# Residual stream in DRAM and a ring of five tiles in the norm stages, in place of a resident tensor

## The chip, the cores and the metric

One core of one Trainium2 chip runs one program. The metric is the device time of one execution in microseconds (us). A core has a matrix engine (TensorE, PE in the profile, with its weight loads as PEld), VectorE (DVE), ScalarE (ACT), GpSimd (POOL) and SyncE (SP), which here only issues DMAs. DMAs that SP issues are in queue q1 of the profile, the indirect gathers that GpSimd issues in queue q0, and both run on the same 16 DMA engines.

## The reference

Two layers of a diffusion backbone over 1024 latent and 256 context tokens of width 1024, all in float32. Cut to what matters here:

```python
for i in range(2):
    hl = modulate(rms_norm(xl, norm_mix[i]), mod_l[0], mod_l[1])   # hc from xc likewise
    yl, yc = neighbourhood_attention(hl, hc, ...) if i == 0 else diff_attention(hl, hc, ...)
    xl = xl + mod_l[2] * yl
    hl = modulate(rms_norm(xl, norm_ffn[i]), mod_l[3], mod_l[4])
    y = grouped_moe(hl, ...)                # layer 0: latent and context tokens, layer 1: latent only
    xl = xl + mod_l[5] * y
return rms_norm(xl, final_norm)
```

`xl` and `xc` together are the residual stream. It is touched in five places only: before each attention, after each attention (the branch is added, then the second norm), and after each mixture of experts, where the addition belongs to the next norm.

## The kernel before, in words

The tokens stand in tiles of 128 partitions by 1024 floats, 512 KB each: ten tiles in all, of which eight are latent. The residual stream `x_res` holds all ten tiles on chip from its allocation in `build` (L1599) to the end, 40 KB of every partition.

One function, `normed`, is called five times, each time as a block of its own with a barrier at its end:

- **Stage 1** (layer 0, mode mix, source None, ten tiles): loads the input into `x_res` and normalises it.
- **Stage 2** (layer 0, mode ffn, source project, ten tiles): projects the attention output, adds it to the stream, normalises, routes.
- **Stage 3** (layer 1, mode mix, source combine, ten tiles): gathers each token's two expert results, adds them, normalises.
- **Stage 4** (layer 1, mode ffn, source project, eight tiles): as stage 2.
- **Stage 5** (mode final, source combine, eight tiles): as stage 3, and the normalised rows are the output.

Between them stand attention, routing and the experts, which do not touch the stream.

Inside a stage every engine has its own written-out program over steps u. In step u, tile u gets its addition, tile u-1 its sum of squares and its 1/rms, tile u-2 its scaling and shift, and tile u-3 its transposes, tile u-4 its routing. The order on each engine:

- **SyncE** issues, in a combine stage, the gate rows (L346; two DMAs of 512 KB in stage 3, one in stage 5), then the norm rows (L360, four DMAs in stages 2 and 3, two in stage 4; L356, one, in stage 5). In an ffn stage `router_w` follows (L377, 64 KB in small pieces). In stage 3, once two tiles are squared, it issues three weight loads of the next attention (L299). In ffn and final stages it then stores each tile's normalised rows as they become ready (L382), and waits for these stores (L384).
- **TensorE**, in an ffn stage, waits for `router_w` and the output weights before its first instruction; then per step 16 matmul calls (L400, 32 in the profile's counts), the transposes (L412) and the router (L420). In stages 1 and 3 it runs four pieces of the next attention's projection between the transposes (L292).
- **VectorE**, in a combine stage, waits for the gate rows before anything. Per tile it combines the two expert rows (L476), multiplies by the gate (L478), adds the result to x (L480), and scales tile u-2 (L501). In an ffn stage it multiplies the projection by its gate (L488).
- **ScalarE** scales the first gathered row (L445), squares (L456) and evicts half of the transposes (L463).
- **GpSimd** issues two indirect gathers of 512 KB for each tile in a combine stage (L523), two tiles ahead, into three buffers; tile t's gather waits until tile t-3 is added. In an ffn stage it adds the two halves to x (L537). It computes 1/rms (L542, L544) and adds the shift (L551).

VectorE's program holds, in a combine stage:

```python
dve.wait_ge(s_gr, 16 * streams)                       # gate rows, before step 0
...
nc.vector.tensor_tensor(x[:, u, :], x[:, u, :], y0, ALU.add).then_inc(s_x, 1)
```

Of the kernel before, what the change touches and what calls it, by code (L numbers as in the profile page):

```python
# [116 lines left out]
def build(nc, a):  # L117
# [4 lines left out]
    h_dram = dram("h_rows", [NTOK, D])  # L122
    idx_dram = [dram(f"slot_token{l}", [SLOTS[l], 16], I32) for l in range(2)]
# [11 lines left out]
    def sb(c, name, shape, dt=F32):  # L135
        return c.enter_context(nc.sbuf_tensor(unique(name), shape, dt))
# [11 lines left out]
    with top:  # L148
# [152 lines left out]
        def normed(l, mode, T, source, hT=None, rw=None, attn=None, wq=None, w_in=None):  # L301
# [3 lines left out]
            with ExitStack() as c:  # L305
                junk = sb(c, "junk", [P, D])
                hr = sb(c, "hr", [P, 3, D])
                if mode == "ffn":
                    hT = sb(c, "h_tile_T", [P, KD, 2 * P])
# [4 lines left out]
                if source is None:  # L314
                    loads = ((0, 2), (2, 5), (5, LT), (LT, NT))
                    s_xin = [sem(c, f"x_in{n}") for n in range(len(loads))]
                    s_toep = sem(c, "toep_out")
                if mode != "final":
                    s_tr, s_eva, s_evd, s_rt, s_rw = (sem(c, n) for n in (
                        "h_transposed", "hT_low", "hT_high", "routed", "router_in"))  # L320
# [20 lines left out]

                @block.sync
                def _(sp):
                    if source == "combine":
                        for v in range(streams):
                            sp.dma_start(gate[:, v, :], mods[prev, v, 5 * D:6 * D].partition_broadcast(P)).then_inc(s_gr, 16)  # L346
# [31 lines left out]
                    if mode != "mix":  # L378
                        for t in range(T):
                            sp.wait_ge(s_h, t + 1)  # L380
                            dst = out[0, t * P:(t + 1) * P, :] if mode == "final" else h_dram[t * P:(t + 1) * P, :]
                            sp.dma_start(dst, hr[:, t % 3, :]).then_inc(s_st[t % 3], 16)  # L382
                        for n in range(3):
                            sp.wait_ge(s_st[n], 16 * len(range(n, T, 3)))  # L384
# [56 lines left out]
                def _(act):  # L441
                    for u in step_range:
# [3 lines left out]
                        if at(u, L_SQ):  # L446
                            t = u - L_SQ
                            if t:
                                act.wait_ge(s_ss, t)
                            if source is None:  # L450
                                for n, (t0, t1) in enumerate(loads):
                                    if t == t0:
                                        act.wait_ge(s_xin[n], 16)
                            else:
                                act.wait_ge(s_x, adds * (t + 1))
                            nc.scalar.activation(junk[:, :], x[:, t, :], ACT.Square, accum_out=ss[:, t:t + 1]).then_inc(s_ss, 1)  # L456
# [10 lines left out]
                def _(dve):  # L467
# [4 lines left out]
                    for u in step_range:  # L472
                        if source == "combine" and at(u, 0):
# [6 lines left out]
                            nc.vector.tensor_tensor(x[:, u, :], x[:, u, :], y0, ALU.add).then_inc(s_x, 1)  # L480
# [9 lines left out]
                        if at(u, L_SC):  # L490
# [10 lines left out]
                            nc.vector.scalar_tensor_tensor(out=hr[:, t % 3, :], in0=x[:, t, :], scalar=rstd[:, t:t + 1],  # L501
# [15 lines left out]
                def _(pool):  # L517
# [11 lines left out]
                    for u in step_range:  # L529
                        if source == "combine" and u + 2 < T:  # L530
                            gather(u + 2)
                        if source == "project" and at(u, 0):
                            for h in range(2):
                                n = 2 * u + h
                                pool.wait_ge(s_g, n + 1)
                                xs = x[:, u, h * HALF:(h + 1) * HALF]
                                nc.gpsimd.tensor_tensor(xs, xs, tmp[:, n % 4, :], ALU.add).then_inc(s_x, 1)  # L537
# [1061 lines left out]
        x = sb(top, "x_res", [P, NT, D])  # L1599
# [50 lines left out]
```

## Time and profile before

| | |
|---|---|
| median of 3 runs | 4670.02 us (4668.69 to 4672.05) |
| the profiled execution: its own time, its span | 4662.88 us, 4661.0 us |
| TensorE busy, mean granted clock | 4244.4 us (91%), 0.956 of full speed |
| VectorE, ScalarE, GpSimd busy | 1412.5, 979.4, 516.2 us |
| DMA | 628.09 MB, mean 135 GB/s over the span |
| stage 1 | 182 to 251 us |
| stage 2 | 1166 to about 1350 us |
| stage 3 | 2427.5 to 2534 us |
| stage 4 | 3481 to 3633 us |
| stage 5 | 4604.8 to 4661 us |

Times inside the span are counted from its first instruction. A row of the timeline gives the start and the length of an instruction or of several merged ones, the engine (SPq is SyncE's queue of DMA issues), the line, what it writes and reads, and in brackets how long the engine had been idle and what ended that. The granted clock is a share of 2.4 GHz: 0.50 is the lower of the two levels.

### The profile page before, as it was taken

The numbers are of one execution on the slowest core, as the hardware profiler recorded it, in microseconds if no ns is written. First come the engines' busy times: TensorE is split into PE (matmuls) and PEld (weight loads), VectorE is DVE, ScalarE is ACT, GpSimd is POOL, SyncE is SP. The second block draws the span as 40 slices with busy tenths as digits, with TensorE's granted clock in tenths as the row PEclk, the third lists the DMA queues.
The fourth block names the chain that finished last, engine by engine and source line by source line (L and its number), as shares of the span: only waits on it lengthen the run. The fifth ranks groups of instructions, "written<-read, shape, count | busy, mean of one in ns | idle before, by whom it ended". The sixth has DMA issues, their size and how long they took to land. (4 is left out here: it accounts for less than half of the span.)

```text
span 4661.0 us, 61468 instructions
## 1 busy us (share of the span) xinstructions
PE 4244.4 (91%) x25164; PEld 3369.6 (72%) x25164; DVE 1412.5 (30%) x2522; ACT 979.4 (21%) x2014; POOL 516.2 (11%) x492
## 2 busy tenths in 40 slices
PE   7799999999967999999975999999989499999994
PEld 2377777777446789999973666666664489999994
DVE  6643333334131101111116444444441311111113
ACT  4433333333000000000112333333331000000102
POOL 0220000000231000000005000000003200000002
PEclk9899999999978999999997999999999699999997
DMA  8770000001135345778852000000010555579894
GB/s 312 247 291 22 22 21 21 21 21 46 37 137 161 128 145 183 240 262 272 294 199 87 14 14 13 13 13 13 13 51 23 186 173 192 196 244 299 296 300 167
DMA packets 468239, 628.09 MB, mean 135 GB/s; under 512 B 30432, under 2 KB 343280, under 8 KB 467928
## 3 DMA queue, kind: packets, MB, share of 16 engines
q1 hardware_dynamic: 439512, 529.33, 34.9%
q0 software_dynamic: 22240, 73.58, 4.4%
q10 hardware_dynamic: 6312, 22.55, 1.2%
q8 instruction: 146, 2.39, 0.2%
q14 instruction: 29, 0.24, 0.0%
HBM read 558.39 MB, written 70.95 MB: 135 GB/s over the span
## 5 line engine op out<-in xcount | busy, mean ns | idle before, releaser
L1507 PE MATMUL ps<-item_xT,expert_ring 128*128 128x128 f32 (+9 forms) x8192 | 1169.6, 306 | 1.1 <-DVE item_xT L1573 1.1
L1507 PEld LDWEIGHTS ps<-item_xT,expert_ring 128*128 128x128 f32 x8192 | 1114.4, 192 | 51.8 <-DVE item_xT L1573 1.4
L1529 PE MATMUL ps<-item_aT,expert_ring 128*128 128x128 f32 (+9 forms) x4096 | 620.2, 307 | 0.0
L1529 PEld LDWEIGHTS ps<-item_aT,expert_ring 128*128 128x128 f32 x4096 | 567.2, 192 | 25.1 <-issue 1.8
L292 PE MATMUL ps<-hT,w_group 128*128 128x512 f32 (+1 forms) x1408 | 532.0, 537 | 6.0 <-ACT df_probs L1092 3.9
L292 PEld LDWEIGHTS ps<-hT,w_group 128*128 128x128 f32 x1408 | 265.7, 191 | 255.1 <-issue 242.7
L1580 DVE TENSOR_TENSOR item_aT<-item_silu,ps 128x128 f32<-128x128 f32 (+9 forms) x256 | 83.8, 327 | 1069.7 <-ACT item_silu L1550 1069.7
L1550 ACT ACTIVATE item_silu<-ps 128x128 f32<-128x128 f32 (+9 forms) x256 | 79.1, 309 | 1137.0 <-PE ps L1507 1137.0
L400 PE MATMUL ps<-hT,oT 128*128 128x512 f32 x576 | 253.9, 601 | 15.9 <-DMA router_w<-in_router_w 15.9
L973 PE MATMUL ps<-df_kT,df_qT 64*128 64x512 f32 (+1 forms) x768 | 257.5, 535 | 0.0
L1588 DVE COPY item_y<-ps 128x512 f32<-128x512 f32 (+3 forms) x106 | 69.0, 684 | 599.9 <-PE ps L1520 599.9
L736 PEld LDWEIGHTS ps<-na_V,rows 128*128 128x128 f32 x1792 | 221.3, 192 | 34.6 <-ACT rows L851 28.9
L736 PE MATMUL ps<-na_V,rows 128*128 128x64 f32 x1792 | 222.3, 273 | 13.0 <-ACT rows L851 12.7
L1457 POOL DMA_INDIRECT gathered<-h_rows,slot_idx x55 | 52.6, 956 | 1543.2 <-PE ps L1490 1532.7
L694 PE MATMUL ps<-na_kT,na_qT 128*128 128x512 f32 (+2 forms) x704 | 219.9, 439 | 0.0
L400 PEld LDWEIGHTS ps<-hT,oT 128*128 128x128 f32 x576 | 110.1, 193 | 150.6 <-issue 150.6
L1553 ACT ACTIVATE item_yT<-ps 128x128 f32<-128x128 f32 (+9 forms) x256 | 79.1, 309 | 627.8 <-PE ps L1529 627.8
L1010 PE MATMUL ps<-df_V,rows 128*128 128x128 f32 x1280 | 184.3, 285 | 23.3 <-ACT rows L1104 20.7
L1092 ACT ACTIVATE df_probs<-ps,df_negmax 128x1280 f32<-128x1280 f32 x128 | 170.1, 1330 | 137.2 <-DVE df_negmax L1163 137.2
L1163 DVE TENSOR_REDUCE df_negmax<-ps 128x1 f32<-128x1280 f32 x128 | 186.4, 1488 | 30.5 <-PE ps L973 28.8
L1010 PEld LDWEIGHTS ps<-df_V,rows 128*128 128x128 f32 x1280 | 157.7, 192 | 47.4 <-issue 23.8
L973 PEld LDWEIGHTS ps<-df_kT,df_qT 64*128 64x128 f32 x768 | 133.2, 186 | 80.9 <-issue 54.4
(196 smaller groups left out, 4198.9 us busy)
## 6 DMA issues: line engine op xcount, KB each, us to landing
expert_ring<-in_expert_w_gate SPq DMA_DIRECT2D x128, 1024.0 KB, 5.3
expert_ring<-in_expert_w_up SPq DMA_DIRECT2D x128, 1024.0 KB, 8.3
expert_ring<-in_expert_w_down SPq DMA_DIRECT2D x64, 2048.0 KB
mod_ring<-in_mod_w SPq DMA_DIRECT2D x24, 2048.0 KB, 10.4
slot_out<-rows POOLq DMA_DIRECT2D x7, 4096.0 KB, 46.8
w_group<-in_w_qkv SPq DMA_DIRECT2D x48, 512.0 KB, 5.3
slot_out<-item_y ACTq DMA_DIRECT2D x35, 512.0 KB, 7.7
h_rows<-hr SPq DMA_DIRECT2D x18, 512.0 KB, 2.6
```

Of the source, the lines that this page charges most:

```text
L292: m = nc.tensor.matmul(dst, wq[:, 0 if kind == "q" else 1, k, :], hT[:, k, c0:c0 + w], start=k == 0, stop=k == KD - 1)
L400: m = nc.tensor.matmul(bank(n % 3), oT[:, k * NTOK + t * P:k * NTOK + (t + 1) * P], wo[:, k, h * HALF:(h + 1) * HALF], start=k == 0, stop= ...
L694: m = nc.tensor.matmul(S(s, c0, c0 + w), qT[:, h, t * P:(t + 1) * P], kT[:, k0:k0 + w], start=True, stop=True)
L736: m = nc.tensor.matmul(O(s), pT[:, s % 2, i * P:(i + 1) * P], V[:, kt, h * HD:(h + 1) * HD], start=i == 0, stop=i == len(ks) - 1)
L973: mm = nc.tensor.matmul(ps[:, c0:c0 + w], qT[r, t * P:(t + 1) * P], kT[r, k0:k0 + w], start=True, stop=True)
L1010: mm = nc.tensor.matmul(O, pT[:, t % 2, i * P:(i + 1) * P], V[:, i, :], start=i == 0, stop=i == NT - 1)
L1092: nc.scalar.activation(pb[:, t % 2 if m == 0 else 2, :], S(m), ACT.Exp, bias=mx[:, 2 * (t % 2) + m:2 * (t % 2) + m + 1], accum_out=ls[:, 2 ...
L1163: nc.vector.tensor_reduce(mx[:, mxcol(t, m)], S(m), AX.X, ALU.max, negate=True).then_inc(s_max, 1)
L1507: m = nc.tensor.matmul(gub(j, b, w), ring[:, b // 2, k, w * 256 + (b % 2) * P:w * 256 + (b % 2 + 1) * P], xT[:, k, 0:C], start=k == 0, sto ...
L1529: m = nc.tensor.matmul(yb(j, d), ring[:, 4 + d // 4, f, (d % 4) * P:(d % 4 + 1) * P], aT[:, f, 0:C], start=f == 0, stop=f == FB - 1)
L1550: nc.scalar.activation(sg[:, b % 2, 0:C], gub(j, b, 0), ACT.Silu).then_inc(s_sg, 1)
L1580: nc.vector.tensor_tensor(aT[:, b, 0:C], sg[:, b % 2, 0:C], gub(j, b, 1), ALU.mult).then_inc(s_a, 1)
```

## The change

The resident tensor goes. The stream is kept in a DRAM tensor `x_rows`, and every stage but the first passes it through a ring of five tiles: SyncE issues five loads at the head of its program, ahead of everything else, stores each tile once it is added (not in stage 5), and loads tile t+5 into tile t's place once that is scaled and its store has landed. Stage 2 loads from the kernel's inputs, so stage 1 stores nothing; stage 1 has all ten tiles in a tensor of its own.

```diff
+    x_dram = dram("x_rows", [NTOK, D])
...
+                XR = T if source is None else 5
+                x = sb(c, "x_tiles", [P, XR, D])
+                store_x = source is not None and mode != "final"
...
+                else:
+                    s_xin = [sem(c, f"x_in{n}") for n in range(XR)]
+                    s_xst = [sem(c, f"x_stored{n}") for n in range(XR)]
...
+                def x_source(t):
+                    if source == "project" and l == 0:
+                        return (a["x"][0] if t < LT else a["ctx"][0])[(t % LT) * P:(t % LT + 1) * P, :]
+                    return x_dram[t * P:(t + 1) * P, :]
+
                 @block.sync
                 def _(sp):
+                    def load_tile(t):
+                        if t >= XR:
+                            sp.wait_ge(s_h if mode == "final" else s_sc, t - XR + 1)
+                            if store_x:
+                                sp.wait_ge(s_xst[t % XR], 16 * (t // XR))
+                        sp.dma_start(x[:, t % XR, :], x_source(t)).then_inc(s_xin[t % XR], 16)
+
+                    if source is not None:
+                        for t in range(min(XR, T)):
+                            load_tile(t)
                     if source == "combine":
...
-                    if mode != "mix":
-                        for t in range(T):
-                            sp.wait_ge(s_h, t + 1)
-                            dst = out[0, t * P:(t + 1) * P, :] if mode == "final" else h_dram[t * P:(t + 1) * P, :]
-                            sp.dma_start(dst, hr[:, t % 3, :]).then_inc(s_st[t % 3], 16)
-                        for n in range(3):
-                            sp.wait_ge(s_st[n], 16 * len(range(n, T, 3)))
+                    if source is not None:
+                        for u in range(T + L_H):
+                            if store_x and u < T:
+                                sp.wait_ge(s_x, adds * (u + 1))
+                                sp.dma_start(x_dram[u * P:(u + 1) * P, :], x[:, u % XR, :]).then_inc(s_xst[u % XR], 16)
+                            if at(u, L_H):
+                                t = u - L_H
+                                if mode != "mix":
+                                    sp.wait_ge(s_h, t + 1)
+                                    dst = out[0, t * P:(t + 1) * P, :] if mode == "final" else h_dram[t * P:(t + 1) * P, :]
+                                    sp.dma_start(dst, hr[:, t % 3, :]).then_inc(s_st[t % 3], 16)
+                                if t + XR < T:
+                                    load_tile(t + XR)
+                        ...
...
-                            nc.vector.tensor_tensor(x[:, u, :], x[:, u, :], y0, ALU.add).then_inc(s_x, 1)
+                            dve.wait_ge(s_xin[u % XR], 16 * (u // XR + 1))
+                            nc.vector.tensor_tensor(x[:, u % XR, :], x[:, u % XR, :], y0, ALU.add).then_inc(s_x, 1)
...
                                 pool.wait_ge(s_g, n + 1)
-                                xs = x[:, u, h * HALF:(h + 1) * HALF]
+                                if h == 0:
+                                    pool.wait_ge(s_xin[u % XR], 16 * (u // XR + 1))
+                                xs = x[:, u % XR, h * HALF:(h + 1) * HALF]
...
-        x = sb(top, "x_res", [P, NT, D])
```

The squaring (L456) and the scaling (L501) index the ring in the same way. At the end of a stage SyncE also waits for the stores of x.

## Rows read from the trace of the kernel before

**Rows 1.** The page's head: the span and its instructions.

```profile
span 4661.0 us, 61468 instructions
```

**Rows 2.** Windows view: opening of stage 1, then of stage 2, and stretches of stages 2, 3, 5.

```profile
core 0: us, PE busy (x) PEld busy (x) DVE busy (x) ACT busy (x) POOL busy (x), PEclk, DMA share, GB/s
186.00:196.00 10.00, 0.00 (x0) 0.00 (x0) 3.27 (x4) 2.30 (x4) 2.69 (x5) 0.50 1.01 393
...
1166.00:1175.00 9.00, 0.00 (x0) 0.01 (x1) 0.00 (x0) 0.00 (x0) 0.00 (x0) 0.50 0.81 240
1175.00:1330.00 155.00, 154.97 (x459) 76.73 (x459) 25.93 (x34) 14.35 (x25) 53.04 (x43) 0.98 0.06 24
...
2455.00:2497.00 42.00, 10.53 (x43) 8.54 (x44) 41.62 (x28) 13.66 (x22) 38.80 (x28) 0.50 0.55 172
...
4620.00:4661.00 41.00, 0.00 (x0) 0.00 (x0) 34.10 (x28) 14.51 (x20) 26.40 (x26) 0.50 0.64 230
```

**Rows 3.** Timeline: SyncE's issues and TensorE's first matmuls in stages 2 and 4.

```profile
1166.18 1.74 SPq L360 DMA_DIRECT2D norm_rows<-mods  x4
1167.97 0.63 SPq L377 DMA_DIRECT2D router_w<-in_router_w  x1
...
1175.03 40.34 PE L400 MATMUL ps<-hT,oT 128*128 128x512 f32 x88 [9.43 <-DMA router_w<-in_router_w]
...
3481.45 0.82 SPq L360 DMA_DIRECT2D norm_rows<-mods  x2
3482.32 0.43 SPq L377 DMA_DIRECT2D router_w<-in_router_w  x1
3487.25 13.03 PE L400 MATMUL ps<-hT,oT 128*128 128x512 f32 x26 [6.45 <-DMA router_w<-in_router_w]
```

**Rows 4.** Timeline of stage 2 around its first normalised tile.

```profile
1219.60 2.23 POOL L537 TENSOR_TENSOR x_res<-x_res,gated 128x512 f32<-128x512 f32 x1 [5.61 <-DVE gated L488]
...
1225.08 0.32 SPq L382 DMA_DIRECT2D h_rows<-hr  x1
```

**Rows 5.** Timeline of the opening of stage 3.

```profile
2427.54 0.82 SPq L346 DMA_DIRECT2D gate_rows<-mods  x2
...
2440.84 1.15 ACT L445 ACTIVATE y_pair<-y_pair,gates 128x1024 f32<-128x1024 f32 x1 [19.41 <-DMA y_pair<-slot_out,slots]
2442.11 1.28 DVE L476 SCALAR_TENSOR_TENSOR y_pair<-y_pair,gates 128x1024 f32<-128x1024 f32 x1 [19.56 <-ACT y_pair L445]
```

**Rows 6.** DMA queues (packets, MB, share): 2427 to 2435, 2435 to 2443, 4604 to 4608.

```profile
q1 hardware_dynamic: 415, 1.56, 52.8%
...
q0 software_dynamic: 467, 1.70, 53.0%
q1 hardware_dynamic: 438, 1.57, 48.7%
...
q1 hardware_dynamic: 187, 0.70, 54.1%
```

**Rows 7.** Timeline of one step of stage 3's steady loop.

```profile
2466.31 1.80 POOL L523 DMA_INDIRECT y_pair<-slot_out,slots  x1 [0.17 <-issue]
...
2468.41 0.95 POOL L523 DMA_INDIRECT y_pair<-slot_out,slots  x1 [0.30 <-issue]
...
2473.84 1.80 POOL L523 DMA_INDIRECT y_pair<-slot_out,slots  x1 [0.17 <-issue]
...
2475.37 1.14 ACT L445 ACTIVATE y_pair<-y_pair,gates 128x1024 f32<-128x1024 f32 x1
...
2477.73 1.28 DVE L476 SCALAR_TENSOR_TENSOR y_pair<-y_pair,gates 128x1024 f32<-128x1024 f32 x1
```

**Rows 8.** Timeline of stage 5: VectorE's first instruction.

```profile
4614.90 1.28 DVE L476 SCALAR_TENSOR_TENSOR y_pair<-y_pair,gates 128x1024 f32<-128x1024 f32 x1 [13.54 <-ACT y_pair L445]
```

**Rows 9.** The chain of waits in stage 5 (start, length, what it was waiting on).

```profile
4626.07 7.63 DMA y_pair<-slot_out,slots
```

**Rows 10.** Tile view of the gathered pairs in stage 3: us to landing.

```profile
DMA to landing us min/median/max: 4.3/5.3/13.3
```

More of the change, by code:

```diff
@@ L377, in _ @@
                         sp.dma_start(rw[:, :, :], a["router_w"].rearrange("(k p) e -> p k e", p=P)).then_inc(s_rw, 16)
-                    if mode != "mix":
-                        for t in range(T):
-                            sp.wait_ge(s_h, t + 1)
-                            dst = out[0, t * P:(t + 1) * P, :] if mode == "final" else h_dram[t * P:(t + 1) * P, :]
-                            sp.dma_start(dst, hr[:, t % 3, :]).then_inc(s_st[t % 3], 16)
-                        for n in range(3):
-                            sp.wait_ge(s_st[n], 16 * len(range(n, T, 3)))
+                    if source is not None:
[11 more added lines that the diff above has]
+                                    load_tile(t + XR)
+                        if mode != "mix":
+                            for n in range(3):
+                                sp.wait_ge(s_st[n], 16 * len(range(n, T, 3)))
+                        if store_x:
+                            for n in range(XR):
+                                sp.wait_ge(s_xst[n], 16 * len(range(n, T, XR)))
                 @block.tensor
@@ L455, in _ @@
                                 act.wait_ge(s_x, adds * (t + 1))
-                            nc.scalar.activation(junk[:, :], x[:, t, :], ACT.Square, accum_out=ss[:, t:t + 1]).then_inc(s_ss, 1)
+                            nc.scalar.activation(junk[:, :], x[:, t % XR, :], ACT.Square, accum_out=ss[:, t:t + 1]).then_inc(s_ss, 1)
                         if mode != "final" and at(u, L_EV):
@@ L500, in _ @@
                             dve.wait_ge(s_rstd, 2 * t + 2)
-                            nc.vector.scalar_tensor_tensor(out=hr[:, t % 3, :], in0=x[:, t, :], scalar=rstd[:, t:t + 1],
+                            nc.vector.scalar_tensor_tensor(out=hr[:, t % 3, :], in0=x[:, t % XR, :], scalar=rstd[:, t:t + 1],
                                                            in1=ab[:, 2 * (t >= LT), :], op0=ALU.mult, op1=ALU.mult
```

## The prediction

> **What bounds the kernel now.** I read the page first: a span of 4661.0 us [rows 1], most of it attention and experts, which never touch the residual stream. So only the five norm stages count, and the question in each is what its opening and its steady loop wait for. The windows view by stage comes next. In stage 2 TensorE is busy 154.97 of 155 us while the DMA engines move 24 GB/s; in stage 3's loop GpSimd is busy 38.80 and VectorE 41.62 of 42 us, at 172 GB/s; stage 5 has DMA at a share of 0.64 and VectorE at 34.10 of 41 us [rows 2]. The timelines show the openings. In both ffn stages TensorE stands still until `router_w` has landed, the last thing that SyncE issues there (idle 9.43 and 6.45 us) [rows 3]; in both combine stages VectorE starts only when the first gathered pair has landed and ScalarE has scaled it [rows 5, 8]. So all four openings are DMA-bound, and three of the loops have room for DMA.
>
> **What the change does to DMA.** It adds 36 loads and 28 stores of 0.524 MB and shortens nothing: no add, norm or matmul gets cheaper, and the 40 KB of each partition that it frees go to no other buffer in the diff. Twenty of the loads are five at the head of each of four stages, 2.62 MB in SyncE's queue ahead of what each opening waits for. The rest is spread over the loops.
>
> **Stages 2 and 4, opening.** The queue keeps its order as far as the rows tell: with four norm rows ahead, matmuls start 8.85 us after the first issue, with two, 5.80 us (1175.03-1166.18, 3487.25-3481.45) [rows 3]. So what is put ahead is paid in full. 2.62 MB go by at what rate? In stage 1, with input tiles, rows and weights queued, the engines moved 393 GB/s [rows 2]: 6.7 us. The ends: 410 GB/s in the busiest stretch ((1.70+1.57) MB in 8 us) [rows 6] gives 6.4, and the difference of the two openings, 3.05 us for 1.05 MB or 344 GB/s, gives 7.6; the window of stage 2's whole opening, start-up included, has 240 GB/s [rows 2], 10.9 us, the far end. I take 6.7, because stage 1's stretch is the one with tiles like these in it. The issue itself (0.43 us each, 1.74 for four [rows 3]) runs under the transfer. TensorE has nothing else to do, and everything after it in the stage is TensorE-bound, so all of it counts: **+6.7 us** twice. TensorE's granted clock is already 0.50 in that wait [rows 2], so a longer one costs no more there.
>
> On the rate the Trainium skill speaks against me: DMA: Bandwidth & Descriptors, in its Specifications, gives HBM about 358 GB/s per core; these rows show 393 and 410, so the measurement decides. By the page's figure the two openings would be 7.3 us each, an estimate, and the sum 1.2 us more.
>
> **Stages 2 and 4, loop.** One step is about 15 us of TensorE work (88 of its matmuls take 40.34 us [rows 3], and the profile shows 32 to a step), and one load and one store are 1.05 MB, 2.7 us at 393 GB/s, against a DMA share of 0.06 [rows 2]. SyncE now waits for the addition of tile u before it stores tile u-2's rows. That order is the one GpSimd has anyway: tile 2's last addition starts at 1219.60 and takes 2.23 us, and the first row store is issued at 1225.08 [rows 4], so the wait is over before. Tile 5's load is issued behind that store and is needed three steps, some 45 us, later. GpSimd's new wait for x is met long before its first add. Nothing: **0**, under cover of TensorE.
>
> **Stage 3, opening.** SyncE's queue q1 now holds 2.62 MB of x, then 1.05 MB of gate rows, for which VectorE waits before its first instruction, then 2.10 MB of norm rows. GpSimd's gathers are in q0 and the engines serve both alike (1.70 and 1.57 MB in the same 8 us) [rows 6]. By 2435, q1 had moved 1.56 MB; from there it gets half of 410 GB/s, 0.205 MB per us. The gate rows are in when 3.67 MB are: 2435 + 2.11/0.205 = 2445.3, and some 0.5 us for the landing, 2445.8. VectorE began at 2442.11 [rows 5], so **+3.7 us**. The first three pairs, 3.15 MB in q0, have their half rate until about 2449, just before VectorE, now later by as much, wants the third. The ends: 0 if q1 gets more than half while the gathers start up, and 7.6 if all five tiles go ahead of the gate rows at 344 GB/s.
>
> **Stage 3, loop.** A step is 7.53 us, from gather to gather (2466.31 to 2473.84), and GpSimd fills it [rows 7]. Into it come a store and a load, 1.05 MB beside the gathers' 1.05 MB; together 5.1 us at 410 GB/s, so they fit. The gathers are issued by 2468.41 and their tile is wanted at 2475.37 [rows 7], 7.0 us later, against a median landing of 5.3 [rows 10], and VectorE takes the pair up only at 2477.73, 1.2 us after ScalarE is done with it [rows 7]: 2.9 us of slack. If both halves of the traffic overlap, the gathers land up to 2.5 us later. I take **0** and keep 2 us for each of six steps, 12 in all, as the far end. x itself is never late: three steps lie between load and addition. The three weight loads that SyncE issues after two tiles hold the first x stores back, but tile 5 is wanted 30 us after the opening. The stage's end, 30 us of TensorE work, does not touch DMA.
>
> **Stage 5.** The same opening: q1 has 2.62 MB of x and 0.52 MB of gate. It had moved 0.70 MB by 4608 [rows 6], and nearly 1.4 by 4610, when the gathers come in; then 1.77/0.205 = 8.6 us to 4618.6, with landing and ScalarE's part about 4619.4 against 4614.90 [rows 8]: **+4.5**. After that DMA is on the path itself: the chain of waits has 7.63 us for tile 4's gather [rows 9], and tile 5's load is issued in it, behind the first output row. 0.52 MB at 410 GB/s: **+1.3**. Tiles 6 and 7 are loaded where VectorE, 34.10 of 41 us busy [rows 2], sets the pace. 5.8 in all; the ends are 2, if q1 gets more than half at the start, and 8.9, which is 7.6 and the 1.3.
>
> **Sum.** 6.7 + 6.7 + 3.7 + 5.8 = 22.9 us. The profiled execution took 4662.88 us, 1.9 more than its span, so it would take 4685.8; the median shown is 4670.02, 7.1 above the profiled one, and I carry the same sum there: **4692.9**, near 4693. Low ends: 6.4 twice, 0 and 2, 14.8 us. High ends without the loop: 10.9 twice, 7.6 and 8.9, 38.3 us, 4708.3.
>
> **Rivals.**
>
> *The loops feel it.* In stage 3 the added traffic makes each gathered pair late by up to 2 us for six steps, and stage 5's later tiles by 1 to 2 us each. For it: stage 5's DMA share is already 0.64 [rows 2], and a gather took 7.63 us once an output row was beside it [rows 9]. Against: 0.55 in stage 3, and the slack above. It decides from 3 us of added landing. 22.9 + 12 + 3 = 37.9, some 4708.
>
> *A slower rate.* The x tiles go at the 344 GB/s of the two ffn openings instead of 393 to 410: 7.6 twice, stage 3's gate rows 2.0 and stage 5's 1.7 us later than above, and 0.2 for tile 5: 22.9 + 1.8 + 2.0 + 1.7 + 0.2 = 28.6, some 4699. For it: the difference in [rows 3]; against: 393 and 410. The 358 GB/s of DMA: Bandwidth & Descriptors in the Trainium skill would put it near here.
>
> *Not slower.* SyncE's DMAs do not hold each other up in order: `router_w` and the gate rows start at once beside the x tiles and only share the engines. `router_w` is 64 KB, so at a fifth of the engines it would lead the queue, TensorE would start as now, and only some 2 us of gather delay would be left: 4672, within the measurement. It decides in the openings of stages 2 and 4: from under 3 us each. For it: nothing in the rows shows two q1 transfers pass each other; against: the 3.05 us that two more rows cost [rows 3].
>
> *The change does not do what it says:* stages that never leave the old path. The diff has none.
>
> **How the numbers follow.** The forecast has 0.78, the slower rate 0.08, the loops 0.08, not slower 0.04, and 0.02 are left for a gain that I can name no mechanism for. The range is 4683 to 4709: it holds the forecast's own ends (4684.8 to 4708.3) and most of the rivals above. A measurement of this kernel tells some 0.2% from no change, 9.3 us; the forecast's low end is above that. Faster 0.02, same 0.05, slower 0.93.
>
> **What the profile would show.** TensorE's first matmul in stages 2 and 4 about 15.5 and 12.5 us after SyncE's first issue, still released by `router_w`; VectorE's first instruction in stage 3 some 18 us after SyncE's first issue, no longer released by ScalarE but by the gate rows; in stage 5 some 14.5 us; the step of stage 3 still 7.5 us and of stage 2 still 15 to 16; DMA up by 33.6 MB to about 662 MB; attention and experts unchanged. I am wrong if matmuls start as before in stages 2 and 4, if stage 3's steps stretch, or if time appears outside the four stages.

## The result, and the profile after

The changed kernel takes 4690.31 us (median of 5 runs, 4688.57 to 4693.73). The kernel before, measured beside it, takes 4668.69 (4661.39 to 4672.05). The ratio is 1.005 with an interval of 1.0036 to 1.0065, so the change costs 17 to 30 us; the medians lie 21.6 apart. The forecast was 4692.9.

The profiled executions differ by a little more: spans of 4661.0 [rows 1] and 4686.8 us, 25.8 apart. The ledger below is made on these two. Head of the page after:

```profile
span 4686.8 us, 61590 instructions
...
DMA packets 477456, 661.66 MB, mean 141 GB/s; under 512 B 31456, under 2 KB 344304, under 8 KB 477144
```

DMA grew from 628.09 to 661.66 MB: all 64 added transfers are there.

**Stages 2 and 4.** Timeline of the kernel after around both openings (start and length in us, engine, line, what it does, number of instructions, idle time before it and what ended that):

```profile
1166.31 2.27 SPq L363 DMA_DIRECT2D x_tiles<-in_x  x5
1168.63 2.28 SPq L384 DMA_DIRECT2D norm_rows<-mods  x4
1170.95 0.44 SPq L401 DMA_DIRECT2D router_w<-in_router_w  x1
...
1181.22 1.19 PE L436 MATMUL ps<-hT,oT 128*128 128x512 f32 x1 [15.50 <-DMA router_w<-in_router_w]
...
3494.37 2.27 SPq L363 DMA_DIRECT2D x_tiles<-x_rows  x5
...
3506.74 8.59 PE L436 MATMUL ps<-hT,oT 128*128 128x512 f32 x14 [13.04 <-DMA router_w<-in_router_w]
```

From SyncE's first issue to the first matmul it is now 1181.22 - 1166.31 = 14.91 us and 3506.74 - 3494.37 = 12.37 us, against 8.85 and 5.80 [rows 3]. The releaser is `router_w` both times. In stage 2 SyncE starts to issue it 4.64 us after its first issue, so the ten us that follow are transfers, not the issue.

**Stages 3 and 5.** Timeline of the kernel after, opening of stage 3 and ends of the first waits in stage 5:

```profile
2434.76 2.53 SPq L363 DMA_DIRECT2D x_tiles<-x_rows  x5
...
2445.97 1.15 ACT L481 ACTIVATE y_pair<-y_pair,gates 128x1024 f32<-128x1024 f32 x1 [17.38 <-DMA y_pair<-slot_out,slots]
...
2452.98 1.28 DVE L512 SCALAR_TENSOR_TENSOR y_pair<-y_pair,gates 128x1024 f32<-128x1024 f32 x1 [23.28 <-DMA gate_rows<-mods]
...
4636.78 1.15 ACT L481 ACTIVATE y_pair<-y_pair,gates 128x1024 f32<-128x1024 f32 x1 [15.74 <-DMA y_pair<-slot_out,slots]
...
4641.13 1.28 DVE L512 SCALAR_TENSOR_TENSOR y_pair<-y_pair,gates 128x1024 f32<-128x1024 f32 x1 [18.98 <-DMA gate_rows<-mods]
```

VectorE was released by ScalarE before [rows 5, 8]; now the gate rows release it, 18.22 us after the first issue instead of 14.57 in stage 3, and 15.82 instead of 10.08 in stage 5. In both, ScalarE has scaled the first pair several us earlier (2445.97 + 1.15 against 2452.98; 4636.78 + 1.15 against 4641.13), so the first gathered row lies there, scaled, and waits for gate rows that stand behind 2.62 MB of x. The chain of waits in stage 5 has the same wait, and the later gather of [rows 9]:

```profile
4627.98 13.13 DMA gate_rows<-mods
...
4656.15 8.30 DMA y_pair<-slot_out,slots
```

**The ledger.** By the start of each stage the kernel after is behind by 2434.76 - 2427.54 = 7.22 us at stage 3, 12.92 at stage 4 (3494.37 against 3481.45), 20.49 at stage 5 (4625.31 against 4604.82).

| where | after minus before, us | forecast |
|---|---|---|
| stage 2 opening | 6.06 | 6.7 |
| stage 3 opening | 3.65 | 3.7 |
| stage 4 opening | 6.57 | 6.7 |
| stage 5 opening | 5.74 | 4.5 |
| rest of stage 5 | -0.4 | 1.3 |
| rest of stage 3, with diff attention | 2.0 | 0 |
| all else (attention, experts) | 2.2 | 0 |

The four openings are 22.0 of 25.8 us. What isn't theirs is looked into by the experiments.

**The loops.** Windows view of the kernel after: the opening of stage 2, a stretch of its loop, stage 3's opening, stage 3's loop:

```profile
core 0: us, PE busy (x) PEld busy (x) DVE busy (x) ACT busy (x) POOL busy (x), PEclk, DMA share, GB/s
1166.00:1181.00 15.00, 0.00 (x0) 0.00 (x0) 0.00 (x0) 0.04 (x1) 0.00 (x0) 0.52 0.89 319
...
1221.20:1261.20 40.00, 40.00 (x119) 19.57 (x118) 8.23 (x10) 4.65 (x8) 18.41 (x14) 1.00 0.25 95
...
2434.80:2453.00 18.20, 0.00 (x0) 0.00 (x0) 0.02 (x1) 2.30 (x2) 5.64 (x6) 0.50 0.95 362
...
2463.00:2505.00 42.00, 9.84 (x40) 7.84 (x40) 40.75 (x28) 16.36 (x23) 38.39 (x30) 0.50 0.96 334
```

Stage 3's loop is the striking row: the DMA share went from 0.55 [rows 2] to 0.96 and the bytes from 172 to 334 GB/s, while VectorE and GpSimd stayed as full as they were (41.62 and 38.80 before). Its step, in the timeline after, is as long as in [rows 7]:

```profile
2491.14 1.80 POOL L560 DMA_INDIRECT y_pair<-slot_out,slots  x1 [0.17 <-issue]
...
2498.69 1.80 POOL L560 DMA_INDIRECT y_pair<-slot_out,slots  x1 [0.17 <-issue]
```

7.55 us against 7.53. In the stretch of stage 2 TensorE is busy for 40.00 of 40 us with four times the DMA beside it.

### The profile page after: what moved, and what is told of

Same layout as the page of the kernel before. It is cut to its first block and busy times, and to the rows that moved or that the text cites. A ratio compares the mean times of both kernels' runs of the same rounds, so it can differ in the third digit from the quotient of the medians.

```text
span 4686.8 us, 61590 instructions
## 1 busy us (share of the span) xinstructions
PE 4249.7 (91%) x25164; PEld 3373.8 (72%) x25164; DVE 1413.1 (30%) x2522; ACT 980.7 (21%) x2014; POOL 515.0 (11%) x492
## 2 busy tenths in 40 slices
DMA packets 477456, 661.66 MB, mean 141 GB/s; under 512 B 31456, under 2 KB 344304, under 8 KB 477144
```

## The experiments

The theory: the price of the ring is what its head loads put ahead of `router_w` and the gate rows in SyncE's queue, at four places, and the traffic in the loops is free. Rivals: the loops' traffic pays part of it; the price is in the bytes and not in their order. "Opening" below is the time from SyncE's first issue to the first matmul (stages 2, 4) or to VectorE's first instruction (3, 5). Ratios are to the kernel before on the same chip.

### The same loads, behind the rows

In stages 2 to 5 the five head loads come after the norm rows, and `router_w` before them. The bytes are the same.

```diff
-                    if source is not None:
-                        for t in range(min(XR, T)):
-                            load_tile(t)
                     if source == "combine":
                         sp.dma_start(gate...)
                     ...  # norm rows
+                    if mode == "ffn":
+                        sp.dma_start(rw[:, :, :], ...)
+                    if source is not None:
+                        for t in range(min(XR, T)):
+                            load_tile(t)
```

> The same 36 loads and 28 stores, but the five head loads are issued after the gate rows, the norm rows and router_w. Theory (the change costs what is queued ahead of router_w and of the gate rows): TensorE's first matmul in stages 2 and 4 is back at about 8.9 and 5.8 us after SyncE's first issue (12.6 us regained), VectorE's first instruction in stage 3 at about 14.6 us (its third, the addition, then waits about 1 us for x), in stage 5 at about 12.5 us, held only by a gather that shares the engines; in all some 17 us less than the changed kernel, near 4673 us, some 4 us above the kernel before. Rival (the bytes themselves cost, wherever they are queued, in the openings or in the loops): within 4 us of the changed kernel, 4686 to 4694 us.

Measured: 4674.97 us, 1.0021 (1.0012 to 1.0031). Timeline of this kernel, stages 2 and 3:

```profile
1165.26 1.74 SPq L381 DMA_DIRECT2D norm_rows<-mods  x4
...
1174.56 1.19 PE L436 MATMUL ps<-hT,oT 128*128 128x512 f32 x1 [9.89 <-DMA router_w<-in_router_w]
...
2445.06 1.23 DVE L517 TENSOR_TENSOR x_tiles<-x_tiles,y_pair 128x1024 f32<-128x1024 f32 x1 [2.12 <-DMA x_tiles<-x_rows]
```

The openings are 9.30, 14.88, 6.41 and 13.48 us, over before's by 0.45, 0.31, 0.61 and 3.40. A new wait has come: the first addition of x in stage 3 is 2.12 us late, because x now stands behind 3.15 MB of rows. With it the sum is 6.9 us, and the ratio says 6 to 14. So order alone takes away 15 of the 22 us of the openings (13.5 of 23.3 by the ratios) with not a byte less, and the rival, by which the bytes cost wherever they stand, is gone except for stage 5. It keeps 3.4 us: there ScalarE releases VectorE again, and it is the gathers that are late, since x runs beside them.

The same kernel once more, to see how far one profile stands for it:

> The kernel of e1_ring_behind_rows once more. Its profiled run took 4664.86 us and agrees with the openings, its other nine runs 4672 to 4680. If the extra 8 to 10 us belong to this order, the median stays near 4675 and a second profile shows in which stage; if it was that chip or that hour, the median comes to 4668 to 4671 us.

4674.2 us, 1.0016 (1.0007 to 1.0026); openings 9.32, 14.76, 6.33 and 13.78, within 0.3 us of the first time. But the spans of the two profiles are 4663.2 and 4674.2. The 11 us between two traces of one kernel lie ahead of stage 2 (3.4), between stage 2's first matmul and stage 3 (2.4), in stage 3 after its opening (4.0) and in the rest: single openings can be compared between traces to about half a us, whole spans can't.

And the changed kernel once more:

> The changed kernel once more, for a second profile and on the chip of e10 and e11. Expected: openings of 14.9, 18.2, 12.4 and 15.8 us again within 0.7 us each; the stretch of stage 3 after VectorE's first instruction, 94.5 us against 92.4 before, is a matter of TensorE's granted clock at its end and differs between runs of one kernel by up to 3 us. Rival (that stretch belongs to the change): again 94 to 95 us with the lower clock.

4687.4 us, 1.0048 (1.0032 to 1.0063); openings 14.83, 17.65, 12.88 and 15.51, together 21.6 over before's, each within 0.6 us of the first profile's. The span is 4683.5 us, 22.5 over before's, so only 0.9 us lie outside the openings here and not 3.8. For the stretch of stage 3 the outcome is the rival's: 94.9 us, again with the lower clock. This run alone doesn't clear the change of it. Others do: the ring of eight takes 92.2 us there and the stores twice 92.5, and the kernel before with `router_w` first, which has no ring, 95.6.

### No traffic in the loops

The head loads stay. No x is stored, no tile is loaded in a loop, tiles 5 to 7 use what lies in the ring, and the head loads read the input x.

```diff
-                store_x = source is not None and mode != "final"
+                store_x = False
-                                if t + XR < T:
-                                    load_tile(t + XR)
-                            dve.wait_ge(s_xin[u % XR], 16 * (u // XR + 1))
+                            if u < XR:
+                                dve.wait_ge(s_xin[u % XR], 16)
```

It leaves out the update of the residual stream between stages. Other values reach the router, and the experts' lists and loads become others; its whole time (4872.09 us) can't be compared, its openings and loops can.

> Leaves out every store of x and every load after the first five of a stage; tiles five and up are added to what lies in the ring, and the head loads of all stages read the input. Theory (the loops hide their traffic): within 3 us of the changed kernel, the whole 25 us of the openings stays; only stage 5 may give back about 1 us, since tile 5's load no longer lies beside a gather. Rival (the ring's traffic in the loops carries a good part of the cost): 8 us or more below the changed kernel, 4682 us or less.

Timeline of this kernel, the first gather of stage 3's loop and the last:

```profile
2510.05 1.74 POOL L559 DMA_INDIRECT y_pair<-slot_out,slots  x1 [13.45 <-DVE x_tiles L516]
...
2553.68 0.94 POOL L559 DMA_INDIRECT y_pair<-slot_out,slots  x1 [0.30 <-issue]
```

Windows view of 42 us of that loop:

```profile
2518.00:2560.00 42.00, 10.83 (x45) 8.83 (x46) 40.92 (x27) 15.65 (x23) 38.61 (x30) 0.50 0.56 176
```

The loop takes 43.63 us here, at a DMA share of 0.56. In the changed kernel the same two gathers are 43.75 us apart, at 0.96:

```profile
2457.05 1.74 POOL L560 DMA_INDIRECT y_pair<-slot_out,slots  x1 [14.41 <-DVE x_tiles L517]
...
2500.80 0.95 POOL L560 DMA_INDIRECT y_pair<-slot_out,slots  x1 [0.30 <-issue]
```

So the loop's traffic costs 0.1 us in stage 3. In the kernel before they are 44.83 us apart. The openings are within 1 us of the changed kernel's, on either side (15.84, 17.22, 12.79, 14.84).

### Every store twice

Each store of x is issued a second time, into a spare buffer: 0.52 MB more in each step.

```diff
                                 sp.dma_start(x_rows..., x[:, u % XR, :]).then_inc(s_xst[u % XR], 16)
+                                sp.dma_start(x_spare[u * P:(u + 1) * P, :], x[:, u % XR, :]).then_inc(s_xst[u % XR], 16)
```

> Each store of x is issued twice, the second time into a DRAM tensor that nobody reads; 14.7 MB more in the loops of stages 2, 3 and 4, openings untouched. Theory (the loops hide what they carry): stages 2 and 4 the same; in stage 3 the engines' share is already 0.96 in the loop, so there the cover runs out and each of some eight steps grows by at most the 0.52 MB at 0.41 MB per us, 1.3 us: 0 to 10 us more than the changed kernel. Rival (each store costs in itself, through SyncE's order or its landing): 28 stores at 1 us or more, in all stages, 25 us or more.

Measured: 4687.23 us, 1.0048 (1.0032 to 1.0063), against 1.005 and 1.0048 for the changed kernel. The rival, a price of each store in itself (25 us or more), is gone. Windows view of this kernel, loops of stages 3 and 2:

```profile
2466.00:2508.00 42.00, 9.84 (x40) 7.85 (x40) 37.31 (x28) 15.70 (x22) 38.40 (x30) 0.50 1.03 400
1215.00:1255.00 40.00, 40.00 (x101) 18.19 (x100) 6.47 (x9) 4.05 (x7) 16.40 (x14) 1.00 0.35 131
```

Timeline, first and last gather of stage 3's loop:

```profile
2459.40 1.74 POOL L562 DMA_INDIRECT y_pair<-slot_out,slots  x1 [14.34 <-DVE x_tiles L519]
...
2504.57 0.95 POOL L562 DMA_INDIRECT y_pair<-slot_out,slots  x1 [0.30 <-issue]
```

Stage 3's loop takes 45.17 us, 1.4 more than in the changed kernel, and VectorE has 37.31 of 42 us instead of 40.75: now DMA is the bound, at 400 GB/s. The changed kernel stands just short of that point. Stage 2's TensorE has no gap in its stretch. Of the loops only stage 3's comes near what the engines can move.

### A ring of eight

All eight tiles are loaded at the head, three more per opening.

```diff
-                XR = T if source is None else 5
+                XR = T if source is None else 8
```

> Ring of eight tiles, so 4.19 MB at each head in place of 2.62. Theory: each opening grows by 1.57 MB at some 0.42 MB per us, 3.7 us in stages 2 and 4, and by 4 to 5 us in stages 3 and 5, where the gathers take half until they are done; in all 16 to 18 us more than the changed kernel, 4706 to 4708 us, although fewer tiles are loaded inside the loops. Rival (what costs is the waiting for a free place of the ring): the same as the changed kernel or faster.

Measured: 4705.71 us, 1.0087 (1.007 to 1.0103). Timeline:

```profile
1188.06 1.19 PE L436 MATMUL ps<-hT,oT 128*128 128x512 f32 x1 [21.11 <-DMA router_w<-in_router_w]
...
3519.18 1.19 PE L436 MATMUL ps<-hT,oT 128*128 128x512 f32 x1 [17.39 <-DMA router_w<-in_router_w]
```

The openings are 20.53, 23.23, 16.72 and 21.99: three more tiles, 1.57 MB, cost 5.6, 5.0, 4.35 and 6.2 us, while five cost 6.06, 3.65, 6.57 and 5.74. The price grows with what stands ahead, as the theory has it, and the median is within 1 us of the one expected. The openings together grow by 21.2 us, though, and not by 16 to 18, most of the excess in stage 2 (5.6 us in place of 3.7). There the second step is steeper than the first (3.6 us per MB against 2.3). Part of it is a slower start: in the 6 us from the first issue the DMA engines move 234 GB/s here and 297 in the changed kernel, 0.38 MB less or about 1 us, while in stage 4 it is 292 against 295. Why the start is slower in stage 2 is open.

### The head loads in another queue

ScalarE issues them; SyncE's own queue is then as it was before the change.

```diff
 @block.scalar
+                    if source is not None:
+                        for t in range(min(XR, T)):
+                            act.dma_start(x[:, t, :], x_source(t)).then_inc(s_xin[t], 16)
```

> The five head loads are issued by ScalarE, in a DMA queue of their own, at the same moment; SyncE's queue begins with the gate rows, the norm rows or router_w as before the change. Theory (order inside one queue, and equal shares between queues that have work): stage 4's first matmul comes when 1.1 MB of SyncE's queue and as much of the other are in, some 3.6 us earlier than in the changed kernel; stage 2's about 1 us earlier, as there SyncE's queue holds nearly as much as the other; stage 3's VectorE starts some 4 us earlier, stage 5's about 1; in all 8 to 11 us less, near 4681 us. Rival (only the total of bytes counts, the engines serve by time of issue): no difference over 2 us from the changed kernel.

Measured: 4684.59 us, 1.0043 (1.0029 to 1.0058). In place of 8 to 11 us less than the changed kernel, the ratios say 3 and the openings together 2.9. The openings of stages 3 and 5 fell to 16.04 and 14.05, and in stage 5 the gate rows land 5.4 us after their issue and not 13.1. Those of stages 2 and 4 did not fall: 15.48 and 12.85. Here the theory, as it was worded, fails: nothing stands ahead of `router_w` in its queue but the norm rows, and it is late all the same. Timeline of stage 4:

```profile
3495.62 0.81 SPq L381 DMA_DIRECT2D norm_rows<-mods  x2
3495.64 3.26 ACTq L477 DMA_DIRECT2D x_tiles<-x_rows  x5
3496.49 0.43 SPq L398 DMA_DIRECT2D router_w<-in_router_w  x1
...
3508.47 1.19 PE L433 MATMUL ps<-hT,oT 128*128 128x512 f32 x1 [13.52 <-DMA router_w<-in_router_w]
```

The DMA queues (packets, MB, share of the engines) tell why; the stretches are 3503 to 3505, 3505 to 3507 and 3507 to 3509:

```profile
q10 hardware_dynamic: 219, 0.78, 95.7%
q1 hardware_dynamic: 218, 0.03, 9.3%
...
q10 hardware_dynamic: 204, 0.75, 94.8%
q1 hardware_dynamic: 297, 0.02, 10.4%
...
q1 hardware_dynamic: 516, 0.03, 17.6%
q10 hardware_dynamic: 29, 0.07, 8.9%
```

In the first stretch, where both have work, the packet counts are equal, 219 and 218, but the bytes are 0.78 and 0.03 MB. That is what it gives if the engines take the two queues in turn, one packet each. `router_w` is 64 KB in 1024 pieces of 64 bytes, and an x tile's packets have 3.6 KB on average (0.78 MB by 219), so each small piece waits for a big one. As q10 runs dry, towards 3507, q1 gets ahead (297 to 204), and after 3507 it goes at its own pace. This agrees with the Trainium skill, DMA: Bandwidth & Descriptors, section Queues, rings and completion order, by which an engine goes round the queues that have work, a packet at a time. A queue of its own helps the gate rows (4 KB rows: half of the bandwidth) and not `router_w`. Nor is the opening all of it: stage 3, from its first issue to VectorE's last scaling, takes 92.2 us here, 92.4 in the changed kernel and 89.4 before, so nearly all of the 2.2 us that its opening gained is lost again in its loop.

### `router_w` first

If small pieces are what suffers, they should go ahead of everything. First in the kernel before, with no ring:

```diff
+                    if mode == "ffn":
+                        sp.dma_start(rw[:, :, :], ...)
                     ...  # norm rows
-                    if mode == "ffn":
-                        sp.dma_start(rw[:, :, :], ...)
```

> The kernel before, with router_w issued ahead of the norm rows in stages 2 and 4. Theory (TensorE waits for whatever lies ahead of router_w in its queue, in the kernel before as well): first matmul about 3 us after SyncE's first issue in both stages, in place of 8.85 and 5.80, so 8 to 9 us less than the kernel before, ratio about 0.998. Rival (another wait, such as the gate rows of the projection or the output weights, or a fixed latency of router_w's small pieces, holds TensorE): under 3 us.

Measured: 4655.67 us, 0.998 (0.9971 to 0.9989), openings 3.59, 14.93, 2.47 and 10.05. Timeline:

```profile
1169.45 2.90 PE L400 MATMUL ps<-hT,oT 128*128 128x512 f32 x3 [4.18 <-DMA router_w<-in_router_w]
```

The first issue is at 1165.86. TensorE starts 5.3 and 3.3 us earlier; the norm rows are wanted only after the first tile's matmuls. So the kernel before had the same fault, in small.

Then the ring in the same manner: `router_w` first in stages 2 and 4 and then x; in stages 3 and 5 gate rows, tiles 0 and 1, norm rows, tiles 2 to 4.

```diff
-                    if source is not None:
+                    if mode == "ffn":
+                        sp.dma_start(rw[:, :, :], ...)
+                    if source == "project":
                         for t in range(min(XR, T)):
                             load_tile(t)
                     ...  # gate rows
+                        load_tile(0)
+                        load_tile(1)
                     ...  # norm rows
+                    if source == "combine":
+                        for t in range(2, XR):
+                            load_tile(t)
```

> The changed kernel with the same DMAs in the order of their need: router_w, ring, norm rows in stages 2 and 4; gate rows, two tiles, norm rows, three tiles in stages 3 and 5. Theory: stages 2 and 4 start about 3 us after the first issue (12 and 9 us less than in the changed kernel), stage 3 at about 15, stage 5 at about 13 us; in all 25 us less than the changed kernel and 4 to 6 us less than the kernel before, though the stream still goes through DRAM. Rival (the ring has a price that no order takes away): 5 us or more above the kernel before.

Measured: 4659.04 us, 0.9987 (0.9978 to 0.9996); openings 2.34, 13.85, 2.51 and 13.70. With the ring and all its bytes the kernel is now faster than the one before. Left over is stage 5, 3.6 us above before: x is in nobody's way in SyncE's queue any more, but it runs beside the first gathers; the next run tests whether that is the cause.

### The ring, paced

The same, with one wait more in stages 3 and 5: after tile 0, SyncE issues nothing until ScalarE has scaled the first pair.

```diff
                         load_tile(0)
+                        sp.wait_ge(s_m, 1)
                         load_tile(1)
```

> As e7_ring_ordered, but in stages 3 and 5 SyncE issues only the gate rows and tile 0 at first and waits until ScalarE has scaled the first gathered row before it issues the rest, so that the first gathers have the engines to themselves. Theory (in the combine stages the opening is the time of the first pair of gathers in competition with SyncE's queue): stage 3 starts about 10 us after the first issue in place of 14.6 to 15, stage 5 at about 10.5, so 4 and 2 us less than e7_ring_ordered, 10 us less than the kernel before. Rival (the bytes held back are missed later: norm rows and tiles 1 to 4 come late and the second and third tile wait): no gain over e7_ring_ordered.

Measured: 4657.11 us, 0.9984 (0.9975 to 0.9993). Timeline of stage 3 and of stage 5's first instruction on VectorE:

```profile
2421.64 0.82 SPq L372 DMA_DIRECT2D gate_rows<-mods  x2
...
2432.95 0.32 SPq L363 DMA_DIRECT2D x_tiles<-x_rows  x1
...
2433.05 1.28 DVE L518 SCALAR_TENSOR_TENSOR y_pair<-y_pair,gates 128x1024 f32<-128x1024 f32 x1 [16.47 <-ACT y_pair L487]
...
2446.81 1.23 DVE L523 TENSOR_TENSOR x_tiles<-x_tiles,y_pair 128x1024 f32<-128x1024 f32 x1 [3.79 <-DMA x_tiles<-x_rows]
...
4605.25 1.28 DVE L518 SCALAR_TENSOR_TENSOR y_pair<-y_pair,gates 128x1024 f32<-128x1024 f32 x1 [13.36 <-ACT y_pair L487]
```

Openings 3.97, 11.41, 2.65 and 10.19: stage 3's is now 3.2 us shorter than before the change, stage 5's equal. That stage 5's falls by 3.5 us against the run before shows that x beside the gathers was what it paid for. But the rival has a part too: the bytes held back are missed later. In stage 3 the addition of the third tile, at 2446.81, waits 3.79 us for x, and from the first issue to VectorE's last scaling the stage takes 87.9 us, against 89.7 in the run before and 89.4 before the change: 1.5 us of the 3.2 are left. The medians of the ordered and the paced ring, 4659.04 and 4657.11, and their ratios don't tell the two apart. Both are faster than the kernel before.

The same order and pace without the ring, on the kernel before (`router_w` first, and `sp.wait_ge(s_m, 1)` ahead of the norm rows in stages 3 and 5):

> The kernel before with both edits of e9_ring_paced and no ring: router_w ahead of the norm rows in stages 2 and 4, and in stages 3 and 5 the norm rows held back until ScalarE has scaled the first gathered row. It shows what the ring itself still costs once the order is right. Theory (nothing but what tile 0 and later tiles take from the gathers): stage 3 starts about 9 to 10 us after the first issue, 1 to 2 us earlier than e9_ring_paced, stage 5 at about 9.5; in all 1 to 3 us less than e9_ring_paced, near 0.998 of the kernel before or just under. Rival (the ring has a price in the loops that the openings hid): 5 us or more less than e9_ring_paced.

Measured: 4649.81 us, 0.9962 (0.9949 to 0.9976), the fastest of all; openings 3.55, 10.18, 2.35 and 9.22. Against the paced ring that is 2.9 us less in the openings; the two profiled spans are 4651.2 and 4651.6 us. The openings are not all, since only the ring has the late addition: up to VectorE's last scaling stage 3 takes 84.8 us here and 87.9 there, 3.1 less, and with the 1.7 of the other three openings the traces show 4.8 us. The ratios differ by 0.0022, some 10 us (3 to 18 with both intervals taken together), and they come from different chips. So the ring, once ordered and paced, costs about 5 us by the traces and 10 by the ratios. That is more than the 1 to 3 of the theory and what the rival asks for; how much it is within 3 to 18 us is open.

### All runs together

The first column is the sum of the four openings over that of before, each from one profile, and in brackets with the wait of an addition for x, where there is one; the second is (ratio - 1) x 4665 us, with its interval.

| kernel | openings, us | by the ratio, us |
|---|---|---|
| ring of eight | 43.2 | 40.6 (33 to 48) |
| changed | 22.0 | 23.3 (17 to 30) |
| changed, again | 21.6 | 22.4 (15 to 29) |
| stores twice | 22.0 | 22.4 (15 to 29) |
| ScalarE's queue | 19.1 | 20.1 (14 to 27) |
| behind the rows | 4.8 (6.9 with x) | 9.8 (6 to 14) |
| the same, again | 4.9 (7.2 with x) | 7.5 (3 to 13) |
| ring ordered | -6.9 | -6.1 (-10 to -2) |
| before, `router_w` first | -8.3 | -9.3 (-14 to -5) |
| ring paced | -11.1 (-7.3 with x) | -7.5 (-12 to -3) |
| before, ordered and paced | -14.0 | -17.7 (-24 to -11) |

Every sum (with x's wait, where there is one) lies in the interval of its ratio. From 43 us slower to 14 us faster, the openings are the effect, within intervals that are 4 to 8 us wide on either side.

## Why the prediction was right

**The mechanism.** All four openings grew, and by the waits that were named: `router_w` twice, the gate rows in place of ScalarE twice. The four terms sum to 21.6; they measured 22.0 here and 21.6 in the second profile. That the sums are so close is in part luck: stage 2's term was 0.6 too large and stage 5's 1.2 too small.

**Stages 2 and 4, 6.7 each.** They measured 6.06 and 6.57, and 5.98 and 7.08 in the second profile: 2.62 MB at 433, 399, 438 and 370 GB/s, around the stretch of stage 1 that was chosen (393) and the busiest one (410). Once the opening contains the five tiles, the whole window reads 319 GB/s instead of 240 [rows 2]: the start-up, not the rate, made the far end. The slower rate is not borne out: 344 GB/s wanted 15.2 for the two, and they took 12.6 and 13.1. The difference between two openings, from which it came, was the weakest basis.

**Stage 3, 3.7.** It measured 3.65 and 3.1. The halving of the engines that this term rests on is there; DMA queues of the kernel after, 2443 to 2452:

```profile
q0 software_dynamic: 484, 1.79, 54.3%
q1 hardware_dynamic: 484, 1.76, 48.0%
```

It holds in bytes only because both sides have packets of the same size. For `router_w` beside x tiles it would have misled, as the run with ScalarE's queue shows; the forecast had no need of it there, since they shared a queue.

**Stage 5, 4.5 and 1.3.** The opening measured 5.74 and 5.43, so this term was 1 us too small, and 1.3 for tile 5 too large: the gather in the chain is longer by 8.30 - 7.63 = 0.67 us, and the stage after its opening comes out 0.4 shorter in all. The sum for the stage, 5.3 against 5.8, is right by two errors that offset.

**The loops, 0.** Right: the loop of stage 3 is 0.1 us from that without traffic, and it takes another 0.52 MB a step, half as much traffic again, to add 1.4. The slack read from [rows 7] was real, though the share went to 0.96 and not, as an average of 5.1 in 7.5 us has it, to 0.7. The rival in which the loops feel it was worth 12 us there and is gone for the change as it stands. In the paced ring, where the bytes come later, the loop does feel them.

**Not slower.** Gone: transfers of one queue held each other up at every opening, and moving `router_w` from last to first is worth 3.3 to 5.3 us even without the ring.

**What the sum lacks.** By the ledger 2.0 + 2.2 us lie outside the openings, where no term stood for them, and time outside the four stages was one of the prediction's own signs of being wrong. It isn't one here: in the second profile only 0.9 us lie outside the openings. The 2.0 are in stage 3, behind its opening. Windows view of the kernel after, a stretch of TensorE work that closes the stage:

```profile
2531.40:2547.40 16.00, 15.83 (x34) 6.65 (x32) 0.69 (x1) 0.01 (x1) 0.00 (x0) 0.88 0.00 0
```

and of the kernel before, the same 34 matmuls:

```profile
2520.30:2534.30 14.00, 13.95 (x34) 5.95 (x32) 0.69 (x1) 0.41 (x1) 0.00 (x0) 1.00 0.00 0
```

They take 15.83 us at a granted clock of 0.88, and 13.95 at 1.00. The 0.88 is a mean; the clock was at its lower level in this stretch of the kernel after:

```profile
2528.50:2535.00 6.50, 5.34 (x13) 3.28 (x14) 0.69 (x1) 0.60 (x1) 1.10 (x1) 0.50 0.00 0
```

This isn't the ring's: from VectorE's first instruction to the next block's first issue, before takes 92.4 us and after 94.5, but two profiles of one kernel (the loads behind the rows) 93.7 and 97.7, and the kernel before, ordered and paced and with no ring, 95.0. From VectorE's last scaling to TensorE's last matmul it is 17.3 us in the four profiles whose clock stays at 1.00 (one has no ring), and 19.0 to 20.3 in those with a part at 0.50 (two have no ring). What sets the clock level in one execution and not in the next was not found. The medians, 21.6 us apart, don't show these 4 us: they are of the one profiled execution.

## What to carry to other kernels

In this kernel a prefetch was free in a loop that another engine bounds, and was paid in full at a stage's opening, where it stood ahead of the one transfer that everybody waits for. So order the loads at a stage's head by when each is wanted: here that is worth about 30 us (the changed kernel against the ordered ring, 23.3 + 6.1), more than the ring costs. In the kernel without a ring, order and pace are worth 17.7 us. Where the loads are in another queue than what is waited for, order doesn't reach them. They can be held back until the first data has arrived, but ask when each is then missed: in stage 5 holding back gained 3.5 us, in stage 3 half of its gain came back as a late addition. And measure a stage to the end of its loop, not its opening alone.

## What the hardware showed

- **Queues share by the packet, not by the byte.** 219 and 218 packets, 0.78 and 0.03 MB, in the same 2 us. A transfer of 64-byte pieces beside one of 4 KB rows has no use from a queue of its own; first in the only queue with work, the same 64 KB let TensorE start 2.3 to 4.0 us after the first issue, instead of 12.4 to 14.9 behind the x tiles and 12.9 to 15.5 in a queue of its own beside them.
- **A DMA share of 0.96 need not slow anything.** Stage 3's loop kept its 7.55 us step at 334 GB/s. At a share of 1.03 and 400 GB/s it did stretch, by 1.4 us in 44.
- **Gathers and plain loads meet at the opening.** 2.62 MB of x beside the first gathers and behind the gate rows cost stage 5 3.4 to 3.7 us (three runs), and 0.1 once it was held back until the first pair was there.
